# The first tiles of two feed-forward stages taken from the residual stream, with the gain in the weights and the root applied to the tiles

## What is computed

```python
def rms_norm_2(x, g):
    xf = x.astype(jnp.float32)
    y = xf * lax.rsqrt(jnp.mean(xf * xf, axis=-1, keepdims=True) + EPS)
    return (y * g.astype(jnp.float32)).astype(x.dtype)
```

## Time and profile before

| what | value |
|---|---|
| median of three runs | 2749.92 us (2745.89 to 2753.32) |
| the profiled execution | 2748.43 us |
| its span in the profile | 2746.3 us |
| TensorE busy | 2671.5 us, 97% of the span |
| VectorE busy | 1324.5 us, 48% |
| ScalarE busy | 624.3 us, 23% |
| GpSimd busy | 304.2 us, 11% |
| granted TensorE clock, mean | 0.984 of full speed |
| `ffn_a` begins, `ffn_b` begins | 1774.80 us, 2330.24 us of the span |

### The profile page before, as it was taken

How to read it: one execution, slowest core, us unless ns; L and a number is a source line. 1 busy time by engine, 2 the same in 40 slices (tenths; PEclk the granted TensorE clock), 3 DMA queues, 4 the chain that set the end, 5 groups by cost and what they waited for, 6 DMA issues and landing times.

```text
span 2746.3 us, 31907 instructions
## 1 busy us (share of the span) xinstructions
PE 2671.5 (97%) x12396; PEld 1853.9 (68%) x12396; DVE 1324.5 (48%) x2846; ACT 624.3 (23%) x1152; POOL 304.2 (11%) x305
## 2 busy tenths in 40 slices
PE   8999999999999999999999998999999999999998
PEld 4777658898895655444444445588874484888887
DVE  2255556656642012000012775467766673777733
ACT  1155542312311112100011134221220022221201
POOL 0222134433432410000000000000000000000000
PEclk9999989999999998999999998999999999999999
DMA  4211111101013220344433210122223311222222
GB/s 188 77 47 62 47 46 47 47 32 47 35 43 109 97 77 29 140 173 174 164 107 107 75 48 16 69 92 78 92 93 107 107 49 55 84 92 81 88 92 92
DMA packets 32494, 226.98 MB, mean 83 GB/s; under 512 B 3552, under 2 KB 4192, under 8 KB 6112
## 3 DMA queue, kind: packets, MB, share of 16 engines
q1 hardware_dynamic: 30384, 219.50, 22.4%
q10 hardware_dynamic: 1968, 5.51, 0.6%
HBM read 222.90 MB, written 2.10 MB: 82 GB/s over the span
## 4 chain that ended last, share of the span: by engine, by line
PE 92%; DVE 5%; ACT 2%; issue 1%; POOL 0%; DMA 0%; DVEq 0%; ACTq 0%; POOLq 0%
PE psum L400 90%; DVE work L2703 1%; PE psum L897 1%; PE psum L1224 0%; DVE work L1800 0%; PE psum L2572 0%; PE psum L2246 0%; DVE hT L572 0%; PE psum L2058 0%; DVE work L1048 0%; DVE work L1794 0%; DMA mixT<-x_dram 0%; ACT work L611 0%; PE psum L634 0%; ACT work L975 0%
## 5 line engine op out<-in xcount | busy, mean ns | idle before, releaser
L400 PE MATMUL psum<-hT,ring 128*128 128x256 f32 (+3 forms) x2968 | 581.2, 376 | 10.9 <-ACT work L1349 6.1
L400 PEld LDWEIGHTS psum<-hT,ring 128*128 128x128 f32 (+2 forms) x2968 | 392.6, 163 | 166.6 <-issue 114.6
L400 PE MATMUL psum<-work,ring 128*128 128x512 f32 (+1 forms) x1208 | 418.5, 498 | 4.8 <-ACT work L3428 2.4
L400 PEld LDWEIGHTS psum<-work,ring 128*128 128x128 f32 x1208 | 228.3, 190 | 178.7 <-issue 156.4
L400 PE MATMUL psum<-work 128*128 128x128 f32 (+7 forms) x2390 | 327.0, 291 | 11.2 <-ACT work L2664 7.6
L400 PEld LDWEIGHTS psum<-work 128*128 128x128 f32 (+2 forms) x2390 | 275.7, 178 | 62.7 <-issue 32.1
L400 PE MATMUL psum<-work,mixT 128*128 128x256 f32 (+2 forms) x1332 | 290.9, 381 | 2.7 <-DVE work L2155 1.5
L400 PEld LDWEIGHTS psum<-work,mixT 128*128 128x128 f32 (+1 forms) x1332 | 232.7, 183 | 50.3 <-issue 16.9
L400 PE MATMUL psum<-ring,work 128*128 (+1 forms) x568 | 248.7, 596 | 2.2 <-issue 1.9
L400 PE MATMUL psum<-xT,ring 128*128 128x256 f32 x1024 | 242.5, 382 | 1.5 <-ACT mixT L752 1.3
L400 PEld LDWEIGHTS psum<-xT,ring 128*128 128x128 f32 x1024 | 188.2, 190 | 33.7 <-issue 6.4
(11 more groups left out here) (444 smaller groups left out, 2747.9 us busy)
## 6 DMA issues: line engine op xcount, KB each, us to landing
ring<-stream_dram SPq DMA_DIRECT2D x204, 1024.0 KB, 4.7
con<-consts_dram SPq DMA_DIRECT2D x1, 2953.0 KB, 13.3
mixT<-x_dram ACTq DMA_DIRECT2D x4, 512.0 KB, 6.5
work<-x_dram ACTq DMA_DIRECT2D x4, 512.0 KB, 6.2
out_dram<-mixT SPq DMA_DIRECT2D x4, 512.0 KB, 3.7
work<-p_dram ACTq DMA_DIRECT2D x1, 512.0 KB, 4.0
con<-ssm_dram ACTq DMA_DIRECT2D x1, 512.0 KB, 3.7
vec<-vecs_dram SPq DMA_DIRECT2D x1, 378.0 KB, 6.0
```

Of the source, the lines that this page charges most:

```text
L400: ins = self.eng.matmul(out, lhsT, rhs, start=start, stop=stop)
```

## The change

- **The first fill of w_up** in both stages is multiplied by the norm's gain in its slot of the ring, by GpSimd (`gained_fill_pool`), two instructions of 128 x 1024. TensorE waits for `gained_fill` in place of `loaded`.
- **The first two tiles** are computed from `xT`, not from `hT` (`first_pair_pe`), so they are not yet multiplied by the root. Product `k` of the first tile waits for chunk `k` of the stream (`chunk_added` in `ffn_a`, `chunk_mixed` in `ffn_b`). `norm_sum_pe` at the end of the mixers is gone: the column sums come after product 1 (`ffn_a`) or product 3 (`ffn_b`) of the first tile, the root rows one product later. The three unread products are gone at both places.
- **The root** is applied by VectorE when it takes the tiles out of PSUM (`rooted`, in place of ScalarE's copies), between the third and the fourth `h_sums` and after the fourth. ScalarE copies the root bank to SBUF (`rstd`) for this.
- **The first four weight sums** are issued before VectorE waits for the stage, ahead of the eight normalizing instructions (`first_sums_dve`).
- `hT` is still made, for the 21 fast passes; product 0 of the first pass waits for it (`h_ready`).

The norm at the other stages is unchanged.

```diff
@@ mixer_pe, ssm_pe
-            norm_sum_pe(e)
@@ ffn_pe
-        def ffn_pe(e, before_last=None, closing=False):
-            e.eng.wait_ge(S[e.landing()], e.landed())
+        def first_pair_pe(e, gain, x_ready, sums_after=1):
+
+            fill_at[gain] = e.c["fill"].n
+            e.eng.wait_ge(S["gained_fill"], e.c["gained_fill"].next())
             w = e.slot(ring)
+            free = e.c["tile"].n
             for half in range(2):
-                e.eng.wait_ge(S["tile_free"], e.c["tile"].at(-1))
-                e.dense(e.bank(), blocks(w, 8 * half, 8), [hT[:, k, :] for k in range(DC)], h_ready if half == 0 else None)
+                e.eng.wait_ge(S["tile_free"], free + half - 1)
+                o = e.bank()
+                for k in range(DC):
+                    if half == 0:
+                        x_ready(e, free, k)
+                    ins = e.mm(o, blk(w, 8 * half + k), xT[:, k, :], k == 0, k == DC - 1)
+                    if half == 0 and k == sums_after:
+                        total_pe(e)
+                    if half == 0 and k == sums_after + 1:
+                        e.eng.wait_ge(S["col_root"], e.c["col_root"].next())
+                        root_rows_pe(e, root_bank, 0).then_inc(S["stage"], 1)
+                ins.then_inc(S["tile_done"], 1)
+
+        def chunk_added(e, free, k):
+
+            e.eng.wait_ge(S["tile_free"], free + k + 1 - DC)
+
+        def chunk_mixed(e, free, k):
+
+            if k == 0:
+                e.eng.wait_ge(S["glu_sig"], DC - 1)
+                e.eng.wait_ge(S["glu_mul"], DC - 1)
+            e.eng.wait_ge(S["x_chunk"], DC + k + 1)
+
+        def ffn_pe(e, gain, x_ready, before_last=None, closing=False):
+            first_pair_pe(e, gain, x_ready, 3 if closing else 1)
...
+                if j == 0:
+                    e.c["h_ready"].n += DC
+                    e.eng.wait_ge(S["h_ready"], e.c["h_ready"].at())
                 product(0, a11, b11)
...
+                else:
+                    e.eng.wait_ge(S["root_out"], e.c["root_out"].next())
                 product(4, a12, b21)
@@ new, GpSimd and VectorE
+        def first_sums_dve(e):
+
+            for i in (0, 2, 1, 3):
+                weight_sum_dve(e, e.c["fast"].n, 0, i)
+
+        def gained_fill_pool(e, gain):
+
+            f = fill_at[gain]
+            e.eng.wait_ge(S["loaded%d" % (f % RING)], 16 * (f // RING + 1))
+            for half in range(2):
+                w = ring[:, f % RING, DC * P * half:DC * P * half + DC * P].rearrange("p (k n) -> p k n", k=DC)
+                ins = nc.gpsimd.tensor_tensor(w, w, bc(V(gain), P), ALU.mult)
+            ins.then_inc(S["gained_fill"], 1)
@@ ffn_act
-            for half in range(2):
-                e.eng.wait_ge(S["tile_done"], e.c["tile"].next())
-                nc.scalar.activation(fpad[:, half, 2:2 + T], e.result(), ACT.Copy).then_inc(S["tile_free"], 1)
-                e.eng.wait_ge(S["tile_free"], e.c["tile"].at())
+            e.eng.wait_ge(S["h_ready"], DC * (NORMS.index(gain) + 1))
+            nc.scalar.activation(rstd, root_bank, ACT.Copy).then_inc(S["root_out"], 1)
+            e.skip(2)
@@ ffn_dve
+            def rooted(half):
+                e.eng.wait_ge(S["tile_done"], e.c["tile"].next())
+                nc.vector.tensor_tensor(fpad[:, half, 2:2 + T], e.result(), rstd, ALU.mult).then_inc(S["tile_free"], 1)
+
...
+                if i == 3:
+                    e.eng.wait_ge(S["root_out"], e.c["root_out"].next())
+                    rooted(0)
                 nc.vector.tensor_tensor(h_sums[:, o, :, :], in0, in1, ALU.subtract).then_inc(S["h_sum"], 1)
+            rooted(1)
...
-            for i in (0, 2, 1, 3):
-                weight_sum(0, i)
@@ the vector program, after norm_root_dve (ffn_a) and after ssm_dve (ffn_b)
+            first_sums_dve(e)
@@ the GpSimd program, at its end
+            e.eng.wait_ge(S["vec_in"], 16)
+            gained_fill_pool(e, "ffn0")
+            gained_fill_pool(e, "ffn1")
```

More of the change, by code:

```diff
@@ L2938, in ffn_pe, with weight_sum_dve, ffn_act @@
             norm_sum_pe(e)
[L2940 removed]
+        def weight_sum_dve(e, n, j, i):
+            f = fill_at[n] + j
+            w = ring[:, f % RING, :]
+            a11, a12, a21, a22 = (w[:, 512 * q:512 * q + 512] for q in range(4))
+            ws = w_sums[:, j % 2, :, :]
+            if i == 0:
+                e.eng.wait_ge(S["loaded%d" % (f % RING)], 16 * (f // RING + 1))
+            if j >= 2:
+                e.eng.wait_ge(S["seven"], 7 * (n + j - 2) + 6)
+            o, in0, in1, op = ((0, a21, a22, ALU.add), (1, ws[:, 0, :], a11, ALU.subtract),
+                               (2, a11, a21, ALU.subtract), (3, a12, ws[:, 1, :], ALU.subtract))[i]
+            if i in (1, 3):
+                e.eng.wait_ge(S["w_sum"], 4 * (n + j) + i)
+            nc.vector.tensor_tensor(ws[:, o, :], in0, in1, op).then_inc(S["w_sum"], 1)
+        def first_sums_dve(e):
[3 more added lines that the diff above has]
+            f = fill_at[gain]
+            e.eng.wait_ge(S["loaded%d" % (f % RING)], 16 * (f // RING + 1))
+            for half in range(2):
+                w = ring[:, f % RING, DC * P * half:DC * P * half + DC * P].rearrange("p (k n) -> p k n", k=DC)
+                ins = nc.gpsimd.tensor_tensor(w, w, bc(V(gain), P), ALU.mult)
+            ins.then_inc(S["gained_fill"], 1)
+        def ffn_act(e, gain, wname, bname, before_down=None, before_last=None, closing=False):
             n = e.c["fast"].n
             m = e.c["gate_ready"].n
[L2943 to L2947 removed]
+            e.eng.wait_ge(S["h_ready"], DC * (NORMS.index(gain) + 1))
+            nc.scalar.activation(rstd, root_bank, ACT.Copy).then_inc(S["root_out"], 1)
+            e.skip(2)
             for j in range(FC):
@@ L2956, in ffn_act @@
                 for half in range(2):
+                    if j == 0:
+                        e.eng.wait_ge(S["tile_free"], e.c["tile"].at(half - 1))
                     at = 6 * j + 3 * half + 2
@@ L3037, in ffn_dve @@
                 if j == 0:
[L3038 to L3039 removed]
+                    e.eng.wait_ge(S["tile_free"], e.c["tile"].at())
                 else:
@@ L3756, in _ @@
             ssm_pe(e)
-            e.eng.wait_ge(S["stage"], e.c["stage"].next())
+            e.c["stage"].next()
             e.mark("ffn_b")
-            ffn_pe(e, closing=True)
+            ffn_pe(e, "ffn1", chunk_mixed, closing=True)
         @block.scalar
@@ L3802, in _ @@
             e.mark("ffn_b")
-            ffn_act(e, "f1_w", "f1_b", closing=True)
+            ffn_act(e, "ffn1", "f1_w", "f1_b", closing=True)
         @block.vector
```

28 lines of the change are left out of this document (7 added, 21 removed).

## The result

| what | before | after |
|---|---|---|
| median (lowest to highest), 5 runs each | 2746.0 us (2744.53 to 2753.32) | 2732.54 us (2730.48 to 2738.23) |
| profiled execution | 2748.43 us | 2733.26 us |
| its span | 2746.3 us | 2731.1 us |
| granted TensorE clock, mean | 0.984 | 0.987 |

The ratio is 0.9944, 95% interval 0.9926 to 0.9961: faster, by 0.4 to 0.7%. The medians differ by 13.5 us; the forecast was 13.6. That they agree to 0.1 us is luck: the interval stands for 10.7 to 20.3 us.

A forecast was written before the change was run, and what follows sets the result against it. TensorE was taken to bound the kernel, with 92% of the chain; entrance gains of 2.83 us in `ffn_a` and 10.74 in `ffn_b`, 13.6 together, taken from the median 2749.92 gave 2736.3 us, range 2732 to 2742.

The forecast's parts named there:

- the first term of the total: Level of the kernel before, 2749.92 us, the median from which the 13.6 us gain was subtracted.
- VectorE is 2.7 us behind its old place: At the `ffn_b` first pass, VectorE starts 8.0 us earlier while TensorE is 10.7 earlier; second-pass cover falls from 4.7 to 2.0.
- TensorE's stretch: Last mixer product to product 1 of the first pass: 18.2 us at both entrances, gaining 2.83 in `ffn_a`, 10.74 in `ffn_b`.
- the 10.7: Gain at the `ffn_b` entrance: some 3.1 us idle stretch, some 4.8 lower clock, the rest unread products.
- The covers of the sums: Last squares are ready before TensorE's column sums need them at both entrances, the narrower cover being 0.5 us.
- The walk: VectorE's reordered work at the entrances: third token sum ready 0.7 us before product 1 in `ffn_b`, about 2.5 in `ffn_a`.
- GpSimd: Gain on the first `w_up` fill: 5.1 us a fill, hidden by 45 us in `ffn_a` and 35 in `ffn_b`.
- Rival A: Lower clock stays in `ffn_b`: 4.8 us come back, gain 8.8, 2741.1 us; in both stages 2745.9; chance 0.10.
- Rival B: VectorE 3 us late for product 1 in `ffn_b`: TensorE idle 2.3 us, gain 11.3, 2738.6 us; chance 0.06.
- Rival C: Products on `xT` held until the last chunk at both entrances: gain 5.4 us, 2744.5 us; chance 0.06.
- Rival D: GpSimd ends late, TensorE waits for `gained_fill`: slower from T near 42 us a fill, 2767 at T = 51; chance 0.03.

The follow-up runs named there:

- The filled run: Kernel before, with three unread products ahead of the sums at the end of the state-space layer; `ffn_b` entrance 24.37 us against 28.94.
- the run with slow GpSimd: Changed kernel with forty more GpSimd products ahead of the gain in each of the two fills; 2770.86 us in one execution.
- the bare norms: Changed kernel with the mixer's entrance filled, minus unread products in router, mixer and state-space norms; 2739.44 us against that version's median 2729.15.
- sums early: Changed kernel with the column sums after product 1 instead of product 3 in `ffn_b`; entrance 21.44 us, total 2738.01 us.
- the same filled: Changed kernel with `ffn_b` column sums after product 1 and two unread products ahead of them; entrance 19.85 us, total 2741.06 us.
- weight sums back: Changed kernel with the first four weight sums back behind the token sums; entrances 19.16 and 20.38 us, total 2740.98 us.

## Where the prediction held and where it failed

The mechanism and its size at the two entrances held. The step that failed is the first term of the total, the level of the kernel before: the prediction subtracted 13.6 from 2749.92, the median of three runs, where five runs of the same kernel have 2746.0, so 2736.3 was 3.8 us too high. Inside the working, the step "VectorE is 2.7 us behind its old place" failed too. Both are taken up below.

- **TensorE's stretch.** 18.2 us worked out, 18.14 measured, at both places; gains 2.83 and 10.74 against 2.89 and 10.80. The sums (1.70) and the root rows (0.89), both taken from the experts' handover, were exact. What was open of the root's chain was 0.08, where 0.1 was allowed: the starts 2317.47 and 2318.41 are 0.94 apart, for a product of 0.86.
- **What the 10.7 are made of.** The prediction had 3.1 idle, 4.8 clock, the rest unread products. The filled run gives 4.6 for the clock, the run with the unread products put back 2.57 for them, and the wait is 3.2 by the starts of the products. These are 10.4 of the 10.80; in `ffn_a` 0.3 us stay over in the same way, and no run splits them further.
- **The total.** Forecast 2736.3, measured 2732.54. The difference was right and the level was not: the term 2749.92 measured 2746.0 with five runs and 2747.24 with the fifteen beside the later experiments. The prediction allowed for the spread of single runs ("up to 3.7 from the middle"), but not for the middle of three runs being off by as much, and its range 2732 to 2742 reaches only 0.5 us below the measured median; the lowest run, 2730.48, lies outside. The stated own time of the profiled execution, 2734.8, missed 2733.26 by the 1.5 us that were already gone before the mixer.
- **The covers of the sums.** The prediction calls the narrower one 0.5 us. By its own rows it is 0.25 (2319.95 against 2320.20), and 0.24 was measured.
- **VectorE.** The walk came out as worked out but 0.3 us better: cover 1.05, not 0.7, in `ffn_b`, and 2.7 in `ffn_a`, where 2.5 was said. The weight sums, not the root, hold up the normalizing, as the prediction said: L572 begins 0.6 us after the last of them starts. For the second pass the prediction had a cover of 2.0 and it is 4.4. What failed is "VectorE is 2.7 us behind its old place": it was 2.3 behind when it made the next weight sum (2331.91 against 2344.86, TensorE 15.23 earlier), but in the kernel before it then waited 1.52 us for ScalarE's first tap, and that wait took most of it up. The prediction had moved VectorE's whole program as a block.
- **GpSimd.** Sized too large, 5.1 us a fill against 3.75, that is 2.54 us for 128 x 1024 against 1.90. Most of that is the operand: with a column repeated along the row, 128 x 512 takes 1.04 us in the run with slow GpSimd, where the row that was doubled has 1.272. The rest is that twice the columns took less than twice the time (1.90 against 2 x 1.04). Hidden either way, by the covers of 45 and 35 us, which the run with slow GpSimd confirmed. Its lines of GpSimd from 1730 to 1740 us:

```profile
L3004 POOL TENSOR_TENSOR ring<-ring,con 128x512 f32<-128x512 f32 x9 | 9.4, 1042 | 0.7
```

- **Rival A** (the lower clock stays) is refuted by 1.00 at both entrances; the experts' handover was the right row to go by. The section of the Trainium skill cited there ("TensorE: Matmul & The Clock Gate", "A second HAM failure mode: psum-queue depth-cycling"), on a clock that swings when TensorE is idle for short moments between groups of matmuls, did not decide here, since no idle moment was left. With the bare norms, which have such moments, the trace agrees with it: 0.88 in place of 1.00, and 0.59 in place of 0.80.
- **Rival B** did not come, but its price was wrong. It took a wait of 2.3 us to be free of the clock, since it is shorter than 3.08. Waits of 2.07 and 1.37 us cost 1.8 us each on top of themselves. At the 3 us late that B supposed, the gain would, as an estimate from these two runs, have been some 2 us less than stated.
- **Rival C** (the products on `xT` start late) is refuted by the row 2312.33: `xT,ring` follows the last mixer product with no idle time, in `ffn_a` too (1767.85).
- **Rival D** is a real mechanism, with the point from which it costs where the prediction put it; that is seven times the row away, and nothing came near. Its price has a slip: 13.6 us are used up from T near 44, not 42, since 44.1 - 35.3 + 4.8 = 13.6 and `ffn_a` still costs nothing there. That the run with slow GpSimd lost 31.2 us at the two places (5.49 + 17.49 idle, 6.15 + 2.02 by the clock) where the prediction has 31.0 for T = 51 is in part luck: it charged 4.8 for the clock at each.

## What to carry to other kernels

Where a norm stands between two TensorE stages, multiply by the gain in the weights and by the root on the result, and the next stage's first products can run on the raw input while the norm is made; place the sums behind as many of them as the last input needs to arrive. Count the wait on such a chain at more than its length: the waits of 1.37, 2.07 and 3.08 us here were each followed by the lower clock (single waits of 0.51 and 0.86 us cost next to nothing, small waits in a row did cost), and products that nobody reads, put into a wait that is there anyway, made two stretches 4.6 and 3.3 us shorter. Then look at who does the work in that shadow: here VectorE's cover was one microsecond, and the order of four of its instructions was worth 5 us over the two places, 1.9 of them by the clock.

## What the runs showed of the hardware

**GpSimd and VectorE.** VectorE's addition into `xT` with both inputs in SBUF takes 0.69 us. In the changed kernel one of them falls into GpSimd's work, and takes 1.61; the instruction beside it, with one input in PSUM, is unchanged at 0.75. Lines of VectorE by form, the changed kernel from 2277 to 2281 us:

```profile
L3571 DVE TENSOR_TENSOR xT<-xT,work 128x512 f32<-128x512 f32 x1 | 1.6, 1614 | 0.0
L3568 DVE SCALAR_TENSOR_TENSOR work<-psum,vec,work 128x512 f32<-128x512 f32 x1 | 0.8, 751 | 5.6 <-ACT work L3502 5.6
```

And in the run with slow GpSimd, from 2296 to 2330 us:

```profile
L551 DVE TENSOR_TENSOR work<-work 128x512 f32<-128x512 f32 x5 | 7.1, 1416 | 0.2
L3579 DVE TENSOR_TENSOR xT<-xT,work 128x512 f32<-128x512 f32 x5 | 5.0, 1007 | 0.2
L3576 DVE SCALAR_TENSOR_TENSOR work<-psum,vec,work 128x512 f32<-128x512 f32 x5 | 3.8, 751 | 20.3 <-ACT work L3510 20.3
```

The Trainium skill, page "SBUF — State Buffer", section "Who interferes with whom", says that a VectorE instruction with two SBUF inputs contends with a GpSimd instruction that reads SBUF; its section "Summary: rules for kernel authors" adds that the second one waits until the first is done. The trace agrees, with 0.9 us of delay for the one instruction of 0.69 (it began at 2279.78, inside GpSimd's second product, and ended at 2281.39, 0.55 after that product), 0.3 and 0.7 on average in the run with slow GpSimd, and none for the one that reads PSUM. It costs nothing here: the stretch that holds it takes 526.34 us, 526.42 in the kernel before, where GpSimd is idle, and 526.38 with the slow GpSimd.

**The same instructions in the same order, in three lengths.** From the first mixer product on `hT` to the last product of the latent-attention mixer, which no experiment touched, TensorE took 250.2 us in four traces (the kernel before, the change, the idle stretch filled in the one and in the other), 253.6 in three (sums early, the same filled, slow GpSimd) and 247.4 in three (weight sums back, unread products back, `ffn_b` alone). In the run with bare norms, which changes this stage's entrance, it was 254.9. The windows 1640 to 1660 and 1660 to 1680 of the run with the sums early:

```profile
1640.00:1660.00 20.00, 18.42 (x82) 11.33 (x81) 17.07 (x56) 7.29 (x22) 0.00 (x0) 0.90 0.00 0
1660.00:1680.00 20.00, 15.12 (x63) 8.97 (x63) 9.19 (x37) 10.99 (x25) 0.00 (x0) 0.83 0.00 1
```

And of the run with the change at `ffn_b` alone:

```profile
1640.00:1660.00 20.00, 18.19 (x92) 11.21 (x91) 18.69 (x59) 7.93 (x24) 0.00 (x0) 1.00 0.00 0
1660.00:1680.00 20.00, 15.06 (x70) 8.93 (x70) 11.85 (x46) 13.12 (x28) 0.00 (x0) 0.93 0.00 1
```

The granted clock differs there, in a stage in which TensorE waits for ScalarE and VectorE again and again; why it falls differently in equal programs, these runs do not show. Such steps of 3 us may be much of the spread between executions, which only the profiled ones could show, while a full stretch such as the 526.4 us between the two entrances repeats to 0.15 us in every run that leaves the state-space layer's entrance alone. That is why the experiments were read from stretches.
